# A hybrid encoder block on one core: expert ring placed over the mixer's buffers, low parts in four pieces, router with 36 stationary columns, scatter inside the branch, loops written out

## What is computed

```python
h = layer_norm(x, ln0_g, ln0_b)
mix = token_mixer(h, ...)            # h @ w_in; 8 heads of a gated delta rule, 16 heads of
                                     # sliding-window attention; concat(o_a, o_b) @ w_o
h = layer_norm(ALPHA * h + mix, ln1_g, ln1_b)
ffn = hierarchical_moe(h, ...)       # group top-1 of 4, then expert top-2 of 8 in the group
h = layer_norm(ALPHA * h + ffn, ln2_g, ln2_b)
```

## Time and profile before

| | us |
|---|---|
| runs | 2224.61, 2225.71, 2225.75; median 2225.71 |
| the profiled execution, all of it | 2223.53 |
| its span | 2221.4 |
| PE busy | 1952.1 (88%) |
| DVE busy | 1197.1 (54%) |
| ACT busy | 587.3 (26%) |
| POOL busy | 347.6 (16%) |

### The profile page before, as it was taken

One profiled execution on the slowest core, in us unless ns is written; L12 is line 12 of the kernel. 1 busy time (PEld: TensorE's weight loads), 2 busy tenths in 40 slices (PEclk: granted clock), 3 DMA queues, 4 the chain that ended last, 5 costly groups with the idle time before them and its releaser, 6 DMA issues.

```text
span 2221.4 us, 24740 instructions
## 1 busy us (share of the span) xinstructions
PE 1952.1 (88%) x9716; PEld 1233.9 (56%) x9716; DVE 1197.1 (54%) x1804; ACT 587.3 (26%) x876; POOL 347.6 (16%) x126
## 2 busy tenths in 40 slices
PE   4799998999999889599979999998988998998991
PEld 3677887787787677488873433333333333333330
DVE  6776567557656255410155554555455554554558
ACT  4233224313322244521131222212221122122211
POOL 1422223123212222034311000000000000000002
PEclk9999999999999999799968999999999999999995
DMA  5421122212122221052189999999999999999981
GB/s 189 152 76 42 53 57 57 57 38 76 38 57 64 58 57 46 31 200 95 57 345 322 404 407 407 406 398 413 406 405 408 405 407 402 407 403 402 412 370 76
DMA packets 171070, 505.43 MB, mean 228 GB/s; under 512 B 16592, under 2 KB 108880, under 8 KB 117488
## 3 DMA queue, kind: packets, MB, share of 16 engines
q1 hardware_dynamic: 167552, 491.61, 58.4%
q0 software_dynamic: 2864, 8.53, 1.4%
q10 hardware_dynamic: 576, 4.19, 0.4%
HBM read 499.97 MB, written 12.72 MB: 231 GB/s over the span
## 4 chain that ended last, share of the span: by engine, by line
PE 48%; DMA 30%; DVE 14%; issue 4%; ACT 2%; SPq 1%; DVEq 0%; POOL 0%; ACTq 0%; POOLq 0%
DMA ring<-in_w_up 29%; PE bank L1971 9%; PE bank L1622 7%; PE bank L1623 7%; PE bank L1624 7%; PE bank L1980 3%; PE bank L1753 2%; PE bank L1940 2%; PE bank L1750 2%; DVE half L1111 2%; PE bank L1742 2%; SPq L551 1%; DVE gd_L L1232 1%; DVE sc L1284 1%; PE bank L1702 1%
## 5 line engine op out<-in xcount | busy, mean ns | idle before, releaser
L1971 PE MATMUL bank<-ring,xbT 128*64 128x512 f32 x2048 | 492.6, 625 | 76.3 <-DMA ring<-in_w_up 75.3
L1493 DVE TENSOR_TENSOR r<-r,bank 128x512 f32<-128x512 f32 x512 | 318.0, 681 | 218.1 <-PE bank L1940 217.6
L586 POOL TENSOR_TENSOR wlo<-raw,whi 128x2048 fp32r<-128x2048 f32 x61 | 283.3, 4645 | 699.6 <-ACT whi L700 473.2
L1971 PEld LDWEIGHTS bank<-ring,xbT 128*64 128x64 f32 x2048 | 156.8, 142 | 364.8 <-issue 363.8
L1622 PE MATMUL bank<-hTh,wlo 128*128 128x512 f32 x720 | 308.6, 429 | 20.0 <-POOL wlo L586 13.9
L1624 PE MATMUL bank<-hTh,whi 128*128 128x512 f32 x720 | 284.6, 395 | 0.0
L1623 PE MATMUL bank<-hTl,whi 128*128 128x512 f32 x720 | 284.6, 395 | 0.0
L970 ACT ACTIVATE yw<-bank,wts_all 64x512 f32<-64x512 f32 x256 | 174.6, 682 | 253.8 <-PE bank L1980 249.8
L1980 PE MATMUL bank<-ring,hidT 128*64 128x512 f32 x1024 | 229.5, 601 | 0.5 <-ACT hidT L963 0.5
L1940 PE MATMUL bank<-yhl,place 128*128 128x512 f32 x512 | 158.1, 429 | 12.6 <-DVE r L1493 9.8
L633 POOL DMA_INDIRECT xb<-h_scr,idx_tok x32 | 30.8, 963 | 879.5 <-PE bank L1947 867.8
(11 more groups left out here) (307 smaller groups left out, 2234.5 us busy)
## 6 DMA issues: line engine op xcount, KB each, us to landing
ring<-in_w_gate SPq DMA_DIRECT2D x128, 1024.0 KB, 28.8
ring<-in_w_up SPq DMA_DIRECT2D x128, 1024.0 KB, 29.1
ring<-in_w_down SPq DMA_DIRECT2D x128, 1024.0 KB, 28.7
raw<-in_w_in SPq DMA_DIRECT2D x45, 1024.0 KB, 5.6
raw<-in_w_o SPq DMA_DIRECT2D x16, 1024.0 KB, 5.0
xt<-in_x SPq DMA_DIRECT2D x4, 1024.0 KB, 9.5
h_scr<-xt SPq DMA_DIRECT2D x4, 1024.0 KB, 4.3
r<-h_scr SPq DMA_DIRECT2D x1, 4096.0 KB, 13.7
```

What stands on the lines that cost most here:

```text
L586: pool.tensor_tensor(wlo[sl][:, :, :].rearrange("p k n -> p (k n)"), raw[sl][:, :], whi[sl][:, :, :].rearrange("p k n -> p (k n)").bitcast ...
L1493: dve.tensor_tensor(v, v, comb_bank(q, tt)[:, :], ALU.add).then_inc(comb_done, 1)
L1971: i = mm(GU[SLOTS * h:SLOTS * (h + 1), :], xT_[:, k, :], w[:, kk * F:(kk + 1) * F], start=k == 0, stop=k == KD - 1)
```

## The change

1. The ring's buffers get an order (`ring_at`) in which the mixer frees its memory: parts of `mxh`, `mxl` and of the strips' buffers. SP no longer waits for the whole projection, but for each group: loads 0 and 1 wait for three pieces before the projection's end, load 2 for a low part, 3 for two pieces before the end, 5 for a low part, 6 for one piece before, 10 for the end, 14 for the logits. `g2` and `b2` stay at the ring's places 12 and 13.
2. `lo` makes the low part in four instructions of 128x512; only the last raises `strip_lo`.
3. The router has `wr` as the stationary operand (36 columns) and `h1T` as the moving one; even k go to partitions 0 to 35 of a bank, odd k to 64 to 99. The bank alternates by tile. ACT (tiles 0 and 1) or DVE (2 and 3) copies the 100 partitions back into `h1T`; when all are there, PE multiplies each by `fold`, two identities above each other, which adds the halves and transposes. ACT's row scalings move behind all copies; DVE scales the last tile.
4. The gathers are issued one after another; the eight scatters move into the branch for `left > 0`, which isn't taken here.
5. All `Fori` loops with a fixed count become Python loops. The loops of the branch stay. Two semaphores are merged into others (`cw_done` into `par_done`, `gcum` into `small_T`).

```diff
+        ring_at = [mx_hi[0], mx_lo[0], raw_at[1], mx_hi[1], mx_lo[1], raw_at[0], mx_hi[2], mx_lo[2], hi_at[1], lo_at[1],
+                   mx_hi[3], mx_lo[3], hi_at[0], lo_at[0], GD + 16 * KB]
...
-            with sp.Fori(1, HEADS) as it:
+            for it in range(1, HEADS):
...
-            sp.wait_ge(strip_mm, STRIPS + PIECES)
...
+                elif n in (0, 3, 6, 10):
+                    sp.wait_ge(strip_mm, STRIPS + PIECES - 3 + (0, 3, 6, 10).index(n))
+                elif n in (2, 5):
+                    sp.wait_ge(strip_lo, STRIPS + PIECES - 1 + n // 5)
                 elif n == RING - 1:
-                    sp.wait_ge(logits, 1)
+                    sp.wait_ge(logits, TT + 1)
...
-                pool.tensor_tensor(wlo[sl][:, :, :].rearrange("p k n -> p (k n)"), raw[sl][:, :],
-                                   whi[sl][:, :, :].rearrange("p k n -> p (k n)").bitcast(F32),
-                                   ALU.subtract).then_inc(strip_lo, 1)
+                for c in range(4):
+                    part = slice(4 * c, 4 * c + 4)
+                    i = pool.tensor_tensor(wlo[sl][:, part, :], raw[sl][:, :].rearrange("p (k n) -> p k n", k=KD)[:, part, :],
+                                           whi[sl][:, part, :].bitcast(F32), ALU.subtract)
+                i.then_inc(strip_lo, 1)
...
-            for t in range(2):
+            for t in range(E):
                 gather(t)
-            pool.wait_ge(table_zero, 16)
-            pool.wait_ge(rt, RT_DEST)
-            for t in range(TT):
-                for c in range(2):
-                    pool.indirect_dma_start(slot_rows, bass.IndirectOffsetOnAxis(ap=rd[:, t, c:c + 1], axis=0),
-                                            toki[:, t, c, :], None).then_inc(scattered, 16)
-            for t in range(2, E):
-                gather(t)
-            pool.wait_ge(scattered, 16 * 2 * TT)
             pool.wait_ge(rt, RT_ALL)
...
+            def lgT_out(t):
+                act.wait_ge(logits, t + 1)
+                act.activation(h1T[0:SLOTS + GROUPS + E, 0, t * P:(t + 1) * P], lgT_bank(t)[0:SLOTS + GROUPS + E, 0:P],
+                               ACT.Copy).then_inc(lgT_done, 1)
+
             h1_root(0)
             for t in range(TT - 1):
                 h1T_out(t, range(4))
                 h1_root(t + 1)
-                if t < TT - 2:
-                    h1_rows(t)
+                if t:
+                    lgT_out(t - 1)
             h1T_out(TT - 1, range(2))
-            h1_rows(TT - 2)
-            h1_rows(TT - 1)
+            for t in range(TT - 1):
+                h1_rows(t)
+            act.wait_ge(l1_gain, TT + 1)
+            act.dma_start(h1_scr_v[:, TT - 1, :], r1[:, TT - 1, :]).then_inc(h1_stored, 16)
...
+            dve.wait_ge(l1_inv, TT)
+            dve.tensor_scalar(r1[:, TT - 1, :], r1[:, TT - 1, :], rs4[:, TT - 1:TT], None, ALU.mult).then_inc(l1_gain, 1)
+            for t in (2, 3):
+                dve.wait_ge(logits, t + 1)
+                dve.tensor_copy(h1T[0:SLOTS + GROUPS + E, 0, t * P:(t + 1) * P],
+                                lgT_bank(t)[0:SLOTS + GROUPS + E, 0:P]).then_inc(lgT_done, 1)
...
-                    i = mm(B0[:, t * 64:t * 64 + GROUPS + E], h1T[:, k, t * P:(t + 1) * P], wr[:, k, :],
-                           start=k == 0, stop=k == KD - 1)
-                return i
+                    r = SLOTS * (k % 2)
+                    i = mm(lgT_bank(t)[r:r + GROUPS + E, 0:P], wr[:, k, :], h1T[:, k, t * P:(t + 1) * P],
+                           start=k < 2, stop=k >= KD - 2)
+                i.then_inc(logits, 1)
...
+                    W(pe, lgT_done, t - 2)
                     router(t - 1)
-            router(TT - 1).then_inc(logits, 1)
+            pe.wait_ge(lgT_done, 2)
+            router(TT - 1)
+
+            pe.wait_ge(lgT_done, TT)
+            for t in range(TT):
+                i = mm(PA[0][:, t * 64:t * 64 + GROUPS + E], h1T[0:SLOTS + GROUPS + E, 0, t * P:(t + 1) * P],
+                       fold[0:SLOTS + GROUPS + E, :], start=True, stop=True)
+            i.then_inc(logits, 1)
```

More of the change, by code:

```diff
@@ L200, in build @@
         wr = at("wr", GD + 48 * KB, [P, KD, GROUPS + E])
-        ring = [at(f"ring{i}", (HT + 8 * KB * i) if i < 14 else GD + 16 * KB, [P, 4 * F]) for i in range(RING)]
+        mx_hi, mx_lo = [HT + 8 * KB * i for i in range(4)], [HT + 8 * KB * (4 + i) for i in range(4)]
+        raw_at, hi_at, lo_at = ([ST + 8 * KB * (2 * j + i) for i in range(2)] for j in range(3))
+        ring_at = [mx_hi[0], mx_lo[0], raw_at[1], mx_hi[1], mx_lo[1], raw_at[0], mx_hi[2], mx_lo[2], hi_at[1], lo_at[1],
+                   mx_hi[3], mx_lo[3], hi_at[0], lo_at[0], GD + 16 * KB]
+        ring = [at(f"ring{i}", ring_at[i], [P, 4 * F]) for i in range(RING)]
         yw = at("yw", GD, [P, 4, F])
@@ L511, in ring_load @@
                 sp.dma_start(raw[sl_][:, :].rearrange("p (k n) -> p k n", k=k), src).then_inc(raw_loaded[sl_], 16)
-            with sp.Fori(0, 4) as m:
+            for m in range(0, 4):
                 for j in range(2):
@@ L533, in _ @@
             sp.dma_start(wr[:, :, GROUPS:], w_route_expert[0].rearrange("(k p) n -> p k n", p=P)).then_inc(ld_ln1, 16)
-            with sp.Fori(1, 4) as nt:
+            for nt in range(1, 4):
                 o_loads(nt)
-            sp.wait_ge(strip_mm, STRIPS + PIECES)
             def weight_source(e, i):
@@ L613, in _ @@
             iteration(0, gdn=False)
-            with pool.Fori(1, HEADS) as it:
+            for it in range(1, HEADS):
                 iteration(it)
             iteration(HEADS, last=True)
-            with pool.Fori(0, 4) as m:
+            for m in range(0, 4):
                 for j in range(2):
                     lo(2 * m + (Q0 + 1 + j), j)
-            with pool.Fori(0, 3) as nt:
+            for nt in range(0, 3):
                 for kg_ in range(4):
@@ L624, in _ @@
                 lo(O0 + 13 + kg_, kg_ % 2)
-            pool.wait_ge(logits, 1)
+            pool.wait_ge(logits, TT)
             pool.memset(xb[:, :], 0.0).then_inc(table_zeroed, 1)
@@ L655, in _ @@
             with pool.If(left > 0):
+                pool.wait_ge(table_zero, 16)
+                for t in range(TT):
+                    for c in range(2):
+                        pool.indirect_dma_start(slot_rows, bass.IndirectOffsetOnAxis(ap=rd[:, t, c:c + 1], axis=0),
+                                                toki[:, t, c, :], None).then_inc(scattered, 16)
+                pool.wait_ge(scattered, 16 * 2 * TT)
                 with pool.Fori(0, left) as i:
@@ L846, in _ @@
                 tanh(0, j)
-            with act.Fori(1, HEADS) as it:
+            for it in range(1, HEADS):
                 iteration(it)
@@ L886, in _ @@
             out_q(0, 0)
-            with act.Fori(1, 4) as m:
+            for m in range(1, 4):
                 q_hi(m, 0)
@@ L915, in _ @@
                 o_hi(0, kg_)
-            with act.Fori(1, 3) as nt:
+            for nt in range(1, 3):
                 for kg_ in range(4):
@@ L1266, in _ @@
             iteration(0, gdn=False)
-            with dve.Fori(1, HEADS) as it:
+            for it in range(1, HEADS):
                 iteration(it)
@@ L1308, in _ @@
             attend(0, 1)
-            with dve.Fori(1, 3) as m:
+            for m in range(1, 3):
                 attend(m, 0)
@@ L1333, in sums @@
                 return dve.bn_stats(bns4[:, t, bass.ds(nt, 1), :].rearrange("p o c -> p (o c)"), v)
-            with dve.Fori(0, 3) as nt:
+            for nt in range(0, 3):
                 for t in range(TT):
@@ L1779, in _ @@
             k_steps(4, slot(3), 0, KD)
-            with pe.Fori(1, HEADS) as it:
+            for it in range(1, HEADS):
                 feed = steps(it)
-                pe.wait_ge(par_done, 1)
+                pe.wait_ge(par_done, 2)
                 gdn(it, feed)
@@ L1841, in _ @@
                 attend(0, j, q_feed(1, j))
-            with pe.Fori(2, 4) as m:
+            for m in range(2, 4):
                 for j in range(2):
@@ L1868, in _ @@
             project(0)
-            with pe.Fori(1, 4) as nt:
+            for nt in range(1, 4):
                 project(nt)
```

38 lines of the change are left out of this document (22 added, 16 removed).

## The result

The changed kernel takes 2170.64 us (median of 4 runs, 2169.26 to 2173.14), the kernel before 2225.73 (2224.61 to 2226.75): a ratio of 0.9754 with a 95% interval of 0.9737 to 0.9771, so 55.1 us less. The forecast was 2192. The profiled run took 2169.26 us with a span of 2167.3, 54.1 less than before's 2221.4.

A forecast was written before the change was run, and what follows sets the result against it. Experts were taken as bound by the weight stream, attention by a DVE, ACT and PE chain, with GpSimd low parts blocking DVE. The terms summed to -33.5 us: 2225.7 - 33.5 = 2192 us, range 2168 to 2208.

The forecast's parts named there:

- start: Start of the kernel: strip 1's low part in pieces ends later, mostly in idle time; +1.5 us, between -2 and +4.
- rival (a): DVE keeps its turn through a run of operations: 24 us more gained, 2168 us; chance 0.15.
- recurrence, with the loops: Seven recurrence rounds: pieces give 7 x 0.3 = -2.1 us, loops written out -0.9 us.
- transition: Last recurrence round: L1237 ends 2.1 us sooner and PE waits for it; -2.1 us.
- attention: Attention: L1291 waits 0.4 instead of 2.5 us; 12.3 us from six units' PE waits, 2.0 from another; -14.3 us.
- router: Router with 36 stationary columns: overlapping column halves shorten the products, logits at 1135.0 against 1143.4; -8.4 us.
- routing to block 0: Logits to first expert product: early ring loads and a faster gather win only -0.8 us.
- scatter: Expert stage: without the scatters the weight stream regains 6.4 us lost from 1175.5 to 1190; -6.4, between 0 and -8.
- if each has its turn: Recurrence: L1118, q and k each let a piece pass; q about 1 us sooner, k at the old time.
- The alternative that I had priced at -10: Recurrence: L1118 takes no part in the turns, so k comes 1.2 us sooner; -10 us.
- the -10.5 of my own bound: Router at full clock throughout: -10.5 us instead of -8.4.
- Slower (e): Fixed GpSimd instruction cost makes strips wait: from 2.9 us per piece, 165 us lost, 2350 us; chance 0.02.

The follow-up runs named there:

- e4: Kernel before with only the loops of fixed count written out, the low part whole: 2222.34 us, ratio 0.9985.
- e1: Kernel before with only the low part in four pieces, loops kept: 2195.7 us, ratio 0.9863.
- e2: Changed kernel with the low part whole again: 2200.23 us, ratio 0.9885.
- e9: Changed kernel with all ring loads waiting until the whole projection is done: 2184.83 us, ratio 0.9812.
- e3: Changed kernel with the eight scatters unconditional again, issued behind the second gather: 2177.41 us, ratio 0.9781.
- e10: Changed kernel with the eight scatters unconditional again, issued behind the 16th gather, in the middle of the expert stage: 2185.12 us, ratio 0.9816.

## Why the prediction was right, and where it was not

The range held the time, and all signs but that of the start were right. That it held is in part luck: the time lies 2.6 us inside the lower bound of 2168, and that bound is rival (a), whose mechanism the rows refute. The sum was 20.6 us short of the profiled difference, two thirds of it in two terms. Forecast against measured, by the steps of the prediction:

| step | forecast | measured |
|---|---|---|
| start | +1.5 | -1.9 |
| recurrence, with the loops | -3.0 | -10.1 |
| transition | -2.1 | -2.4 |
| attention | -14.3 | -21.0 |
| router | -8.4 | -10.3 |
| routing to block 0 | -0.8 | -1.0 |
| scatter | -6.4 | -7.4 |

**Recurrence: the step that failed is "if each has its turn".** I let L1118, q and k each give GpSimd a piece, so that k came at the old time. DVE and GpSimd do take turns, and L1118 does take part: L1135 takes 1.25 us beside a piece. (The Trainium skill, VectorE: DVE Perf Modes, Mode 2×_2P, says of such single-source operations between SBUF and SBUF that they use both read ports. The trace agrees in so far as L1135 waits like an operation with two inputs, 1.25 us against 0.17.) But q passes right behind it without a wait. L1135 and q together let one piece pass and not two, so k is one piece, 1.1 us, earlier. Where no L1135 stands there, q waits in its place (1.77 us), and k ends 8.94 us after the start of the reciprocal, as early as behind L1135. In the third round k ends 9.03 us after the start of the reciprocal instead of 10.19, and the next reciprocal starts 77.05 us after it instead of 78.24. So five rounds give -6.1. The fourth (79.1 in the looped kernel, 77.2 now) gives -1.9 and the last (78.0, 75.8) -2.2. These two are the rounds that had the spell of 7 us at 0.50 in the looped kernel, and it is gone or half as long now; e4's last round, without it, shows 1.3. The -0.9 of the loops came: e1 with loops has rounds of 77.20 us, straight code 77.05. With two pieces the same rule gives k at the old time, and the rounds without a spell were 77.9 to 78.3; with eight it gave 75.6, and they were 75.3. Rival (a), DVE keeping its turn through a run, is refuted: k and the copy behind it wait for a piece each. The alternative that I had priced at -10 had the size, but for a wrong reason: it had L1118 not take part. Whether q gets through because L1135 is short or because GpSimd isn't ready for its next piece so soon was not tried.

**Attention: the mechanism was right, its size was not.** L1291 fell to 0.56 us, the six waits went, PE became the bound. The mis-sized term is the price of a wait. I took its idle time, 12.9 us for six. The units lasted 21.2 us on average and last 18.05 now: 19.1 us for six, against 12.3 forecast. The 6 us more are what stands beside it: a spell of lower clock in three units (1.35 us each, by e4), the wait of 0.3 for L1278 at two loop edges, and about 0.2 a unit for PE to get going again (20.11 in e4, less 1.85 of wait, against 18.04), in sum 5.9; another 0.6 is idle time that I hadn't counted. Of the 21.0, e4 shows 5.1 with whole low parts, and e2 15.9 for the pieces on straight code. The seventh unit gave 1.9 for 2.0.

**Start.** The late strip came as forecast (67.43 instead of 60.79), but cost nothing: PE's wait at strip 3 vanished as a whole (6.17 us), and DVE's copy L1106 of the summed decays, which waits for PE behind those strips, starts at 103.97 us instead of 104.19. The term left out is the first round, where a low part held up L1127 too. Its rows, before and after (minimum, median, maximum ns of eight):

```profile
L1127 DVE SCALAR_TENSOR_TENSOR gd_sz<-th,half x8: 683/685/4278, 122.6 to 673.6; 128x512 f32<-128x512 f32 x8
```
```profile
L1144 DVE SCALAR_TENSOR_TENSOR gd_sz<-th,half x8: 682/685/911, 122.0 to 663.8; 128x512 f32<-128x512 f32 x8
```

One operation in eight lasted 4.28 us; I had read medians. The maximum of this row would have shown it. That this operation carries the gain is read from the rows, no run isolates it; e1 shows -1.3 for the pieces as a whole.

**Router.** Column halves overlap, a tile takes 1.95 us (forecast 1.8). The miss is the clock: I let it fall at the last tile as before, and it stayed at 1.00, which is the -10.5 of my own bound.

**Routing.** The number was right, and its reason was incomplete: I priced the early ring loads by what they win, and not by what their absence would cost once the router is 10 us shorter. e9 puts that at 11.8 us in the routing.

**Scatter.** Right, by 0.4 us in e3 (6.8). I had taken the loss at the restart for the whole price. e10 shows that the whole is 14.5 us. The rule that I weighed against this term (the Trainium skill, DMA: Bandwidth & Descriptors, Why small descriptors are slow: some cycles and 32 bytes for each) gives next to nothing for 1024 small rows, and the runs disagree with it: 14.5 us at 406 GB/s are 5.9 MB not moved, 5.7 KB for each row.

**Slower (e)** stayed far off (by its own numbers a piece of 2.9 us would cost 2.5 us a strip, 4 x 2.9 + 1.9 - 11.0, and not 2.7): four pieces take 5.02 us undisturbed, 1.25 each, against 4.60 for one, and the projection kept its 176 us.

## What to carry to other kernels

Where two engines exclude each other for a whole instruction, list every short operation of the critical engine that falls beside a long one of the other, by its maximum and not by its median, and choose the piece's length by that place: here two pieces for the start, where DVE's own operations are long, and eight where they are short (2152.6 us). A wait of PE costs more than its idle time: divide stages by their period, not by their idle rows. And price the parts of a change together: early loads that seem to win 1 us were what 12 us of another part stood on, and a scatter that costs 7 us in one place costs 14 in another.

## What the runs showed of the hardware

- A DVE operation of 12 elements per partition waits for a GpSimd instruction as a large one does: it took 2.30 us beside half a low part and 1.25 beside a quarter (0.17 alone). With four and with eight pieces the operation behind it then passed in its normal 0.68 us.
- GpSimd pays 0.14 us for each added piece (4.60, 5.02 and 5.61 us for one, four and eight), and waits for DVE as well: four pieces took 6.43 us beside L1254, and eight took 8.09.
- Eight scatters of 128 small rows take 14.5 us of a full weight stream while the DMA share stays at 1.00.
- A round of the recurrence in which the granted clock stayed at 0.50 for some 7 us was 0.8 to 1.3 us longer than its neighbours, in loops and in straight code alike: 79.08 against 78.25 before, 78.9 to 79.4 against 78.1 in e4, 79.06 against 77.95 with two pieces. With four and eight pieces the wait ahead of it is at most 1.5 us and no round has such a spell.
